# One expert of the tenth pair is loaded once, into used-up buffers, and the ring of weight slots skips it

## The reference, cut to what matters

```python
h2 = rmsnorm(x, lw['g_norm_ffn']) * (1.0 + scale_f) + shift_f
x = x + gate_f * moe_ffn(h2, lw)
...
gates = sigmoid_topk_gates(hb, lw['w_router'], lw['b_router'])   # 8 of 64 experts for a token
a = jnp.einsum('td,edf->tef', hb, lw['w_e_gate'])                # 64 x 1024 x 256
b = jnp.einsum('td,edf->tef', hb, lw['w_e_up'])                  # 64 x 1024 x 256
routed = jnp.einsum('tef,efd->td', jax.nn.silu(a) * b * gates[..., None], lw['w_e_down'])
```

## Time and profile before

| | us |
|---|---|
| median of 3 runs | 1022.16 (1021.47 to 1022.84) |
| the profiled execution, its own time | 1022.12 |
| its span in the trace | 1020.4 |
| pair 0's first up matmul | 522.43 |
| pair 31's first up matmul | 995.99 |
| TensorE idle before up matmuls, for weights of the ring | 15.5 in 21 pairs |

### The profile page before, as it was taken

The page is one execution under the profiler, slowest core; times in us unless marked ns, Lnnn a source line. Parts: engine busy times, 40 slices in busy tenths (PEclk is TensorE's granted clock), DMA queues, the critical chain, the costliest instruction groups (busy, mean ns, idle before and its releaser), DMA issues.

```text
span 1020.4 us, 14130 instructions
## 1 busy us (share of the span) xinstructions
PE 978.8 (96%) x4558; PEld 551.9 (54%) x4558; DVE 610.4 (60%) x1562; ACT 187.5 (18%) x384; POOL 56.7 (6%) x81
## 2 busy tenths in 40 slices
PE   6999999999999999999999999999999999999997
PEld 2477756544446788888744344444444344344443
DVE  3503322368764010123749889888888888888875
ACT  3311231345435100002510010000000010010000
POOL 0100001000000000000210000000000000000000
PEclk9999999999999999999999999999999999999999
DMA  8995459655536383544468999999999999999992
GB/s 314 419 368 206 173 172 327 207 154 175 169 104 258 127 358 135 206 145 185 169 227 336 417 427 423 426 425 422 425 426 423 424 426 423 425 421 425 423 393 73
DMA packets 53906, 310.66 MB, mean 304 GB/s; under 512 B 8810, under 2 KB 28298, under 8 KB 31842
## 3 DMA queue, kind: packets, MB, share of 16 engines
q1 hardware_dynamic: 47538, 296.13, 73.3%
q0 software_dynamic: 6320, 13.93, 3.9%
HBM read 315.80 MB, written 2.87 MB: 312 GB/s over the span
## 4 chain that ended last, share of the span: by engine, by line
PE 66%; DMA 26%; DVE 3%; issue 2%; SPq 1%; ACT 0%; DVEq 0%; PEldq 0%
PE bank L693 46%; DMA ring<-in_w_e_gu 25%; PE pA L693 15%; PE pB L693 2%; PE pC L693 2%; DMA pT<-in_poolT 1%; PE pD L693 1%; SPq L551 1%; PE pA L728 1%; DMA ring<-in_w_br 0%; PE pA L937 0%; DVE xT L2249 0%; PE pC L946 0%; DVE xT L2325 0%; SPq L414 0%
## 5 line engine op out<-in xcount | busy, mean ns | idle before, releaser
L693 PE MATMUL pA<-ring,qT 128*64 128x512 f32 x1008 | 226.8, 595 | 15.5 <-DMA ring<-in_w_e_gu 15.5
L2237 DVE STREAM_TRANSPOSE qT<-xs 32x256 f32<-32x256 f32 x480 | 209.2, 436 | 7.7
L693 PE MATMUL bank<-hT,ring 128*128 128x264 f32 (+1 forms) x832 | 191.1, 388 | 0.9 <-PE bank L693 0.9
L693 PEld LDWEIGHTS bank<-hT,ring 128*128 128x128 f32 (+1 forms) x832 | 155.4, 189 | 35.1 <-issue 8.7
L693 PEld LDWEIGHTS pA<-ring,qT 128*64 128x64 f32 x1008 | 76.2, 137 | 140.5 <-issue 131.6
L693 PE MATMUL bank<-pT,vtok 128*128 128x264 f32 x512 | 127.9, 393 | 0.3 <-DVE pT L2329 0.3
L693 PEld LDWEIGHTS bank<-pT,vtok 128*128 128x128 f32 x512 | 92.0, 190 | 39.3 <-issue 26.7
L2246 DVE TENSOR_TENSOR pT<-pT,bank 128x264 f32<-128x264 f32 x248 | 100.0, 427 | 8.8 <-PE bank L693 7.3
L693 PE MATMUL bank<-wuk,ring 128*128 128x512 f32 x192 | 86.3, 597 | 0.0
L693 PE MATMUL pB<-ring,oaT 128*64 128x512 f32 x252 | 62.0, 605 | 0.0
L693 PE MATMUL pC<-ring,oaT 128*64 128x512 f32 x252 | 60.4, 592 | 0.0
(11 more groups left out here) (323 smaller groups left out, 779.8 us busy)
## 6 DMA issues: line engine op xcount, KB each, us to landing
ring<-in_w_e_gu SPq DMA_DIRECT2D x63, 2048.0 KB, 23.0
ring<-in_w_e_dn SPq DMA_DIRECT2D x63, 1024.0 KB, 18.5
ring<-in_poolT SPq DMA_DIRECT2D x64, 208.0 KB, 2.7
ring<-in_w_ada SPq DMA_DIRECT2D x12, 1024.0 KB, 9.9
ring<-in_w_bg SPq DMA_DIRECT2D x4, 3072.0 KB, 11.8
ring<-in_w_mix SPq DMA_DIRECT2D x5, 2048.0 KB, 14.7
ring<-in_w_ada SPq DMA_DIRECT2D x4, 2048.0 KB, 13.0
ring<-in_poolR SPq DMA_DIRECT2D x56, 128.0 KB, 2.1
```

What stands on the lines that cost most here:

```text
L693: return nc.tensor.matmul(out, lhsT, rhs, start=start, stop=stop)
L2237: last = V.transpose(xTs[32 * j:32 * j + 32, q % 2, :, 32 * a:32 * a + 32], src[32 * a:32 * a + 32, j])
```

## The change

Expert 19, the second of pair 9, leaves the ring. It is loaded once, in five transfers, into `h2tok`, `hT`, `wrou` and `bsp`, right after expert 4 and before expert 5. Since that overwrites `hT`, its content is first stored to a table in HBM (`h2kept`, 1056 KB) from where the dense fallback would take it back. All later experts move up by one place in the ring: `refill(7)` loads experts 18 and 20 in place of 18 and 19, `refill(8)` 21 and 22, `refill(9)` only 23, and `refill(10)` loads 24 and 25 as before. TensorE's and SP's loops end before pair 9 and begin anew after it. VectorE's and GpSimd's loops stay as they were. The identity's load now counts on another semaphore. The core of the diff:

```diff
+KEPT = 19
+MID = KEPT // 2
 def place(e):
-    return ORDER[(e - 1) % NSLOT], (e - 1) // NSLOT
+    n = e - 1 if e < KEPT else e - 2
+    return ORDER[n % NSLOT], n // NSLOT
...
+        kept_gu = [h2f[:, k * 512:(k + 1) * 512] for k in range(6)] + [hTf[:, k * 512:(k + 1) * 512] for k in range(2)]
+        kept_dn = [[hTf[:, (2 + hf) * 512:(3 + hf) * 512] for hf in range(2)], [wrf, bsf]]
...
-            for b, e in ((3, 3), (2, 4)):
-                reuse(b, "exp")
-                routed(b, e)
+            reuse(3, "exp")
+            routed(3, 3)
+            sp.wait_ge(s["h2s"], 1)
+            sp.wait_ge(s["h2"], DT)
+            sp.dma_start(h2kept, hT[:]).then_inc(d_kept, 16)
+            reuse(2, "exp")
+            routed(2, 4)
+            sp.wait_ge(d_kept, 16)
+            sp.wait_ge(d_tok, 16 * 6)
+            n = BASE["shup1"]
+            sp.wait_ge(full[n % 4], n // 4 + 1)
+            sp.dma_start(h2f, A["w_e_gu"][KEPT][:, 0:6].rearrange("p k c -> p (k c)")).then_inc(d_kept, 16)
+            sp.dma_start(hTf[:, 0:1024], A["w_e_gu"][KEPT][:, 6:8].rearrange("p k c -> p (k c)")).then_inc(d_kept, 16)
+            sp.dma_start(hTf[:, 1024:2048], A["w_e_dn"][KEPT][:, 0]).then_inc(d_kept, 16)
+            sp.dma_start(wrf, A["w_e_dn"][KEPT][:, 1, 0:512]).then_inc(d_kept, 16)
+            sp.dma_start(bsf, A["w_e_dn"][KEPT][:, 1, 512:D]).then_inc(d_kept, 16)
...
             refill(0, None, (5,))
-            with sp.Fori(0, 14) as i:
+            with sp.Fori(0, (MID - 3) // 2) as i:
                 for p in (1, 2):
                     refill(p, i, (2 * p + 4, 2 * p + 5))
-            refill(29, None, (62, 63))
+            refill(MID - 2, None, (KEPT - 1, KEPT + 1))
+            refill(MID - 1, None, (KEPT + 2, KEPT + 3))
+            refill(MID, None, (KEPT + 4,))
+            with sp.Fori(0, (NPAIR - 3 - MID) // 2) as i:
+                for p in (MID + 1, MID + 2):
+                    refill(p, i, (2 * p + 4, 2 * p + 5))
...
+                    elif e == KEPT:
+                        pe.wait_ge(d_kept, 16 * 6)
+                        gu.append(kept_gu)
...
-            with pe.Fori(0, 7) as i:
+            with pe.Fori(0, (MID - 1) // 4) as i:
                 for b in range(4):
                     pair(1 + b, i)
+            pair(MID)
+            with pe.Fori(0, (NPAIR - 2 - MID) // 4) as i:
+                for b in range(4):
+                    pair(MID + 1 + b, i)
```

More of the change, by code:

```diff
@@ L131 @@
 ORDER = (1, 0, 3, 2)
+KEPT = 19
+MID = KEPT // 2
 def place(e):
-    return ORDER[(e - 1) % NSLOT], (e - 1) // NSLOT
-LOADS = [[place(e)[0] for e in range(1, E)].count(b) for b in range(NSLOT)]
+    n = e - 1 if e < KEPT else e - 2
+    return ORDER[n % NSLOT], n // NSLOT
+LOADS = [[place(e)[0] for e in range(1, E) if e != KEPT].count(b) for b in range(NSLOT)]
 def ada_bank(x):
@@ L306, in build @@
         first_gu = [adx[:, k, :] for k in range(CT)] + [kTf[:, k * 512:(k + 1) * 512] for k in range(CT)]
+        hTf, h2f = hT[:].rearrange("p k t -> p (k t)"), h2tok.rearrange("p j c -> p (j c)")
+        wrf, bsf = wrou[:].rearrange("p k e -> p (k e)"), bsp[:].rearrange("p k t -> p (k t)")
+        kept_gu = [h2f[:, k * 512:(k + 1) * 512] for k in range(6)] + [hTf[:, k * 512:(k + 1) * 512] for k in range(2)]
+        kept_dn = [[hTf[:, (2 + hf) * 512:(3 + hf) * 512] for hf in range(2)], [wrf, bsf]]
         first_dn = [[wuk[:, hf, :] for hf in range(2)], [zpf[:, hf * 512:(hf + 1) * 512] for hf in range(2)]]
@@ L353, in build @@
         d_early = [sem(f"early_pages{g}") for g in range(len(EGROUP) - 1)]
-        d_fold = sem("identity_input")
         d_c = sem("conditioning")
@@ L358, in build @@
         d_first = sem("first_expert")
+        d_kept = sem("rows_kept_kept_expert")
         d_tabs = sem("routing_tables")
@@ L380, in build @@
         norms = nc.dram_tensor("head_norms", (2, H, NT), F32, kind="Internal").ap()
+        h2kept = nc.dram_tensor("h2_kept", (P, DT, NT), F32, kind="Internal").ap()
         h2rows = nc.dram_tensor("h2_rows", (NT, D + E), F32, kind="Internal").ap()
@@ L576, in _ @@
                 sp.wait_ge(s["dn1"], NPAIR)
+                sp.dma_start(hT[:], h2kept).then_inc(d_kept, 16)
                 with sp.Fori(0, E // 4) as i:
@@ L592, in _ @@
             nc.gpsimd.memset(csig[:], 0.0).then_inc(s["consts"], 1)
-            pool.dma_start(ident[:], A["ident"]).then_inc(d_fold, 16)
+            pool.dma_start(ident[:], A["ident"]).then_inc(d_late, 16)
             nc.gpsimd.memset(lg[:, 2, :], 1.0).then_inc(s["consts"], 1)
@@ L606, in _ @@
             pool.dma_start(zs[:, 0:2], A["stateT"]).then_inc(d_late, 16)
-            pool.wait_ge(d_late, 16 * 7)
+            pool.wait_ge(d_late, 16 * 8)
             pool.wait_ge(s["ckv"], 1)
@@ L744, in _ @@
             pe.wait_ge(s["csilu"], 1)
-            pe.wait_ge(d_fold, 16)
+            pe.wait_ge(d_late, 16)
             ada_item(0)
@@ L804, in _ @@
             colsum("kvn", sq[:, QT + KT_ + 1, :], 3)
-            pe.wait_ge(d_late, 16 * 7)
+            pe.wait_ge(d_late, 16 * 8)
             ada_item(4)
@@ L1266, in down @@
                         dn.append(first_dn)
+                    elif e == KEPT:
+                        dn.append(kept_dn)
                     else:
@@ L1313, in _ @@
             pair(0)
-            with pe.Fori(0, 7) as i:
+            with pe.Fori(0, (MID - 1) // 4) as i:
                 for b in range(4):
                     pair(1 + b, i)
+            pair(MID)
+            with pe.Fori(0, (NPAIR - 2 - MID) // 4) as i:
+                for b in range(4):
+                    pair(MID + 1 + b, i)
             pe.wait_ge(s["flag"], 1)
             over = pe.value_load(flag[0:1, 0:1], min_val=0, max_val=1)
-            for p in range(29, NPAIR):
+            for p in range(NPAIR - 2, NPAIR):
                 pair(p)
@@ L1324, in _ @@
                 pe.wait_ge(s["fgates"], 1)
+                pe.wait_ge(d_kept, 16 * 7)
                 n = BASE["fgates"]
@@ L1787, in _ @@
             dve.sem_inc(s["varlat"], 1)
-            dve.wait_ge(d_late, 16 * 7)
+            dve.wait_ge(d_late, 16 * 8)
             dve.wait_ge(s["krin"], 1)
```

## The result

The changed kernel takes 1016.88 us (median of 5 runs, 1016.17 to 1016.98) against 1021.93 us for the kernel before (5 runs, 1021.47 to 1022.84). The ratio is 0.9947 (95% interval 0.9932 to 0.9961), so the change gains 5.05 us, half a per cent. The forecast was 1017.1.

A forecast was written before the change was run, and what follows sets the result against it. One gap-free DMA weight stream was taken to set the end: skipping expert 19 gives -7.4 us, its early load +7.4 less 5.0 us of gap (+2.4), so 1022.1 - 5.0 = 1017.1 us, range 1015.2 to 1019.9.

The forecast's parts named there:

- The end is the end of one weight stream: Whole program: ends when one long weight stream is through plus an unchanging tail; gain equals the engine idle time filled.
- The gap is worth 5.0 us: DMA engines, 522 to 546 us: idle 4.1 us by share or 6.9 by bytes; 5.0 us taken.
- Rival (a): Gap at 522 to 546: nearly all of the early load is free, gap worth 6.9 us, 1015.2 us; chance 0.13.
- The early load costs 7.4 us: Expert 19's five queued transfers behind expert 4: 3.146 MB at the gap-free rate, 7.4 us of the engines.
- Rival (d): Expert 19's early load: transfers do not overlap, load takes 20.4 us, slower at 1030.1 us; chance 0.03.
- 2.4 us of delay: Everything behind the early load: 7.4 - 5.0 = 2.4 us later; pair 3's load lands after about 15.6 us.
- the new wait of 0.5 us before pair 8: TensorE before pair 8: lead of 1.8 us minus 2.4 us delay leaves a new wait of about 0.5 us.
- the lead of 1.8 us at pair 8: Weight stream at pair 8, kernel before: the refill's second load lands 1.8 us before 639.15.
- Waits of 15.5 us become 10.5: TensorE's waits for ring weights: 5.2 us before pairs 10 to 16 go, those from about pair 17 stay.
- Rival (c): Early load's queue delays gathers too, or the lead is spent before pair 9: no change, 1021 or so; chance 0.09.
- Rival (e): DMA-paced pairs: shifted slots and gathers give 12 more pairs with a longer wait, slower at 1024 us; chance 0.05.
- a pair period above 15.6 us in the last third: Last third of the pairs: listed sign of being wrong; mean period in the DMA-paced part before was 15.59 us.

The follow-up runs named there:

- e1_late: Changed kernel with expert 19 loaded behind refill(2), in the gap-free stream, instead of behind expert 4: 1022.15 us.
- e3: Kernel before plus two stores of the residual (2.16 MB together) behind expert 4's load, ring unchanged: 1022.38 us.
- e2: Changed kernel plus two stores of the residual (2.16 MB together) behind expert 19's load: 1022.21 us.
- e9_two_after: Changed kernel with a second expert, 37, also out of the ring and loaded behind expert 5: 1017.01 us.
- e11_two_split: e10_split_load with a second expert, 37, also out of the ring and loaded behind expert 5: 1012.43 us.
- e10_split_load: Changed kernel with three of expert 19's transfers (2048 KB) ahead of expert 4, the two into hT still behind it: 1014.50 us.
- e4_before_split: Kernel before with only TensorE's and SP's loops ended before pair 9 and begun anew after it: 1021.92 us.
- e8_no_store: Changed kernel without the store of hT to HBM and without the dense fallback's reload of it: 1016.63 us.
- e5_early: Changed kernel with all five of expert 19's transfers issued ahead of expert 4 instead of behind it: 1015.28 us.

## Why the prediction was right, point by point

- *The end is the end of one weight stream, and the change is worth the idle time that the early load fills.* Shown from three sides: the load put into the gap-free stream gains nothing (e1_late), known work put in the gap costs 0.25 us before the change (e3) and 5.3 us after it (e2, 1016.88 to 1022.21), and a second early expert gains only where the gap has room (e9_two_after, e11_two_split). A load that fits whole into idle time is worth its full 7.4 us (e10_split_load).
- *The gap is worth 5.0 us.* The median gain is 5.05 us, and e3_before_extra, with at least 3.6 us, agrees. The size itself was a choice between two readings, 4.1 us by the share of busy engines and 6.9 by bytes, and no row fixed it. That it came out within 0.1 us is partly luck. Rival (a), which took 6.9 us and 1015.2, is below the fastest of the five runs (1016.17).
- *The early load costs 7.4 us, not 17 or 20.* It took 7.9 us in the trace. Rival (d), each transfer paying its start, needed 12.4 us and is excluded. The row I took it from is the fullest window of expert 0's load; from 378 to 391 the engines moved 408 GB/s, still near it. One of the five issues on SP took 1.42 us and not 0.4, so they ended at 524.5 and not 523.3; SP's next work is at 529.35, and nothing waited for them.
- *2.4 us of delay, and "-7.4 + 2.4" for all that follows.* Right at pair 3 and right in sum. The second load of pair 3's refill landed after 15.6 us, as forecast. And e10_split_load, whose load delays nothing, is 2.4 us faster than the changed kernel (1014.50 against 1016.88). What did not come is the new wait of 0.5 us before pair 8. The second loads of the two refills (changed kernel, issued at 543.1 and 617.1) and, for comparison, that of e4_before_split at 617.8:

```profile
ring<-in_w_e_gu SPq DMA_DIRECT2D x1, 2048.0 KB, 15.6
...
ring<-in_w_e_gu SPq DMA_DIRECT2D x1, 2048.0 KB, 20.8
...
ring<-in_w_e_gu SPq DMA_DIRECT2D x1, 2048.0 KB, 17.6
```

20.8 us is 0.7 us later than in the kernel before (20.1), but 3.2 us later than in e4_before_split, whose ring and loads are those of the kernel before. So the stream's progress up to this point differs by 2.5 us between two traces of the same ring, while from pair 0's up to pair 31's they take 473.6 and 473.5 us. The part that was too fine is the lead of 1.8 us at pair 8: it was read off one execution, and in the changed kernel's there was 1.0 us left. Why the stream's progress differs is open.
- *Waits of 15.5 us become 10.5, from about pair 17.* 10.4 us, from pair 18.
- *Rival (c), the gathers are delayed.* They are (the gather issued near 537.7 landed after 9.6 us, where it took 4.5 before), but no pair waited for one.
- *The store of hT is hidden* and *the split loops cost nothing*: e8_no_store and e4_before_split, both within 0.3 us of their base. The store landed 3.9 us after its issue at 496.98, by 500.9. The changed kernel has three packets on the instruction queue q8 and one on q14 between 600 and 960, where the kernel before has none, without a stop of TensorE. So the rule of the Trainium skill against loops ("Runtime: NRT & Kernel Launch", section "Instruction fetch mechanics") shows no price here.
- *Rival (e), the stream's own pace.* One of my signs of being wrong did come: a pair period above 15.6 us in the last third. From pair 18 to pair 30 the changed kernel takes 188.29 us for 12 pairs, 15.69 each, where the kernel before has 187.10, 15.59. It does not take the change to get there, for e4_before_split, with the ring as before, has 15.76 (us, then busy time of PE, PEld, DVE, ACT and POOL, clock, DMA share, GB/s; changed kernel, e4_before_split):

```profile
787.16:975.45 188.29, 178.17 (x804) 79.12 (x804) 158.77 (x412) 16.55 (x37) 11.88 (x12) 1.00 1.01 424
...
792.56:981.68 189.12, 178.17 (x803) 79.14 (x804) 158.47 (x411) 16.36 (x36) 11.87 (x12) 1.00 1.01 424
```

Pair 18 starts 7.1 us earlier than in the kernel before (794.21) and pair 31 5.9 us. Against this one trace of the kernel before, the changed kernel is further ahead than forecast at pair 18 and loses part of it up to pair 30, so the two deviations partly offset each other; the gain of 5.05 us rests on the medians and not on this pair of traces.

## What to carry to other kernels

Where transfers set the end, ask when the DMA engines last stood idle before the gap-free stretch, and what buffer is free at that moment: work moved out of that stretch into idle time ahead of it is gained byte for byte, up to the size of the gap, and the same work put elsewhere in the stretch is worth nothing. Read the gap off short windows of the DMA share. A dummy transfer of known bytes tests it, but one that fits gives only a lower bound; use one that is too large for the gap as well. A load put into idle time ahead of a latency-bound transfer (here the first gather, which landed after 6.3 us in e5_early and after 4.4 in e10_split_load) must be through before that one starts; split it if it is not.

## What the runs showed of the hardware that was not expected

- Five transfers of 256 to 1536 KB, queued behind each other, ran at the rate of large ones (7.9 us for 3.146 MB). The Trainium skill gives a fixed 2.0 us for each DMA issued by GpSimd ("DMA: Bandwidth & Descriptors", section "Anatomy of one DMA — SWDGE (gpsimd) path"); in this queue of SP no such part adds up.
- Stores of 2.16 MB to HBM took the whole gain of 5.05 us away (e2_after_extra), and loads of the same bytes at 426 GB/s would be an estimated 5.1 us.
- The period into pair 24 is 16.20 us in the kernel before (871.58 to 887.78), in the changed kernel (864.53 to 880.73) and in e4_before_split (870.57 to 886.77), where the one ahead of it is 15.4 to 15.5. It lies between 16.14 and 16.23 us in all 11 traces in which the stream sets the pace there. The changed kernel loads these experts into other slots and 7 us earlier, so the long period goes with the experts' place in HBM or with the pair, and not with the slot. Which of the two is open. The periods into pairs 25, 26 and 30 are less fixed: 15.37, 15.57 and 15.52 us in the kernel before, 15.82, 16.09 and 16.24 in the changed kernel, 16.04, 16.14 and 16.21 in e4_before_split.
